# Experts: the order of a block's gate-and-up products with the high and low parts of the weights

## What is computed

```python
def expert_step(acc, ws):
    wgu, wd, g = ws
    a, b = jnp.split(x @ wgu, 2, axis=-1)
    return acc + g[:, None] * ((jax.nn.silu(a) * b) @ wd), None
```

## Time and profile before

| what | value |
|---|---|
| median of 3 runs | 1197.23 us (1196.26 to 1197.84) |
| the profiled execution's own time | 1197.68 us |
| its span, first to last instruction | 1195.8 us |
| experts' stage, first gate-and-up matmul to last down matmul | about 851.4 to 1160.1 us of the span |
| PE busy over the span | 1155.7 us, 97% |
| HBM traffic | 232.9 MB |

### The profile page before, as it was taken

One profiled execution on the slowest core, in us unless ns is written; L12 is line 12 of the kernel. 1 busy time (PEld: TensorE's weight loads), 2 busy tenths in 40 slices (PEclk: granted clock), 3 DMA queues, 4 the chain that ended last, 5 costly groups with the idle time before them and its releaser, 6 DMA issues. The chain is left out here.

```text
span 1195.8 us, 20090 instructions
## 1 busy us (share of the span) xinstructions
PE 1155.7 (97%) x7096; PEld 1018.7 (85%) x7096; DVE 716.3 (60%) x1262; ACT 597.8 (50%) x1006; POOL 87.2 (7%) x91
## 2 busy tenths in 40 slices
PE   8999999999999999999989999898799999999997
PEld 8999999899999989999979899687688888878862
DVE  3325255254453643535544765556898999989945
ACT  3233344333344334343365733313688888888952
POOL 0000000000000000000000000011222222222113
PEclk9999999999999999999999999898799999999999
DMA  6624316224252162522623333732699999999916
GB/s 200 168 77 120 104 56 168 75 75 133 69 149 76 53 166 75 145 70 62 168 64 105 89 106 120 278 117 111 238 373 358 357 348 368 380 364 370 367 55 263
DMA packets 178475, 210.50 MB, mean 176 GB/s; under 512 B 14054, under 2 KB 141543, under 8 KB 178428
## 3 DMA queue, kind: packets, MB, share of 16 engines
q1 hardware_dynamic: 155440, 188.07, 47.4%
q10 hardware_dynamic: 13644, 10.77, 2.8%
q0 software_dynamic: 9344, 11.03, 2.6%
HBM read 200.19 MB, written 32.71 MB: 195 GB/s over the span
## 5 line engine op out<-in xcount | busy, mean ns | idle before, releaser
L344 PE MATMUL bank_u<-x_hi,w_hi 128*128 128x320 f32 (+1 forms) x1024 | 326.6, 319 | 0.4 <-DVE x_lo L771 0.4
L345 PE MATMUL bank_u<-x_lo,w_hi 128*128 128x320 f32 (+1 forms) x1024 | 318.9, 311 | 0.0
L346 PE MATMUL bank_u<-x_hi,w_lo 128*128 128x320 f32 (+1 forms) x1024 | 318.0, 311 | 0.0
L344 PEld LDWEIGHTS bank_u<-x_hi,w_hi 128*128 128x128 f32 x1024 | 192.5, 188 | 8.7 <-issue 7.0
L345 PEld LDWEIGHTS bank_u<-x_lo,w_hi 128*128 128x128 f32 x1024 | 192.9, 188 | 0.0
L346 PEld LDWEIGHTS bank_u<-x_hi,w_lo 128*128 128x128 f32 x1024 | 192.8, 188 | 0.0
L766 DVE TENSOR_TENSOR w_lo<-w_raw,w_hi 128x1024 fp32r<-128x1024 f32 x80 | 97.8, 1222 | 147.8 <-ACT w_hi L544 147.3
L544 ACT CAST w_hi<-w_raw 128x1024 fp32r<-128x1024 f32 x80 | 83.4, 1043 | 45.6 <-issue 28.4
L1488 PE MATMUL banks<-w_hi_space,xT_hi 128*128 128x512 f32 x256 | 103.4, 404 | 2.0 <-issue 2.0
L1490 PE MATMUL banks<-w_hi_space,xT_lo 128*128 128x512 f32 x256 | 100.3, 392 | 0.0
L1489 PE MATMUL banks<-w_lo_space,xT_hi 128*128 128x512 f32 x256 | 100.3, 392 | 0.0
(11 more groups left out here) (282 smaller groups left out, 2140.8 us busy)
## 6 DMA issues: line engine op xcount, KB each, us to landing
w_raw<-in_w_in SPq DMA_DIRECT2D x64, 512.0 KB, 4.1
first_up<-in_w_gate_up SPq DMA_DIRECT2D x16, 2048.0 KB
second_up<-in_w_gate_up SPq DMA_DIRECT2D x16, 2048.0 KB
first_down<-in_w_down SPq DMA_DIRECT2D x16, 1024.0 KB
second_down<-in_w_down SPq DMA_DIRECT2D x16, 1024.0 KB
k_cache<-in_cache_k SPq DMA_DIRECT2D x16, 512.0 KB
v_cache<-in_cache_v SPq DMA_DIRECT2D x16, 512.0 KB
w_raw<-in_w_branch SPq DMA_DIRECT2D x16, 512.0 KB, 4.3
```

The lines of the kernel that those rows point to most:

```text
L344: pe.matmul(out, w_hi[:, u % 2, k, :], x_hi[:, k, cols], start=(k == 0), stop=False)
L345: pe.matmul(out, w_hi[:, u % 2, k, :], x_lo[:, k, cols], start=False, stop=False)
L346: last = pe.matmul(out, w_lo[:, u % 2, k, :], x_hi[:, k, cols], start=False, stop=(k == KT - 1))
```

## The change

In `gate_up` the 24 matmuls of a block are put into two passes over k. The first pass holds the two products with the high parts of the weights (16 matmuls) and waits for the high parts only (`up_hi_done`). The second holds the product with the low parts (8 matmuls) and waits for the low parts. `up_used` is now reported in the second pass, after the 18th, 20th, 22nd and 24th matmul of the block. No other engine's program is edited.

```diff
                 wait(pe, act_done, j - 1)
                 for k in range(KT):
                     if k % 2 == 0:
+                        pe.wait_ge(up_hi_done, 4 * j + k // 2 + 1)
+                    pe.matmul(bank_g[par][:], xT_hi[:, par, k, :], up_hi[:, k, :], start=(k == 0), stop=False)
+                    pe.matmul(bank_g[par][:], xT_lo[:, par, k, :], up_hi[:, k, :], start=False, stop=False)
+                for k in range(KT):
+                    if k % 2 == 0:
                         pe.wait_ge(up_lo_done, 4 * j + k // 2 + 1)
-                    pe.matmul(bank_g[par][:], xT_hi[:, par, k, :], up_hi[:, k, :], start=(k == 0), stop=False)
-                    pe.matmul(bank_g[par][:], xT_hi[:, par, k, :], up_lo[:, k, :], start=False, stop=False)
-                    last = pe.matmul(bank_g[par][:], xT_lo[:, par, k, :], up_hi[:, k, :], start=False, stop=(k == KT - 1))
+                    last = pe.matmul(bank_g[par][:], xT_hi[:, par, k, :], up_lo[:, k, :], start=False, stop=(k == KT - 1))
                     if k % 2 == 1:
                         last.then_inc(up_used, 1)
```

## The result

| | before | after |
|---|---|---|
| median | 1197.53 us (1196.26 to 1198.68, 4 runs) | 1211.31 us (1209.21 to 1211.47, 4 runs) |
| ratio to before | | 1.011, 95% interval 1.0097 to 1.0123 |
| profiled execution, its span | 1195.8 us | 1209.6 us |

The change makes the kernel slower by 13.8 us. The page of the kernel after, part 1, shows that the same instructions now stand in a longer span. PE has 43 us without work instead of 40, and its busy time grew by 10.9 us although the work is the same. Most of that growth is waiting that the modelled ends cover: in blocks 3 to 28 PE is shown busy for 253.22 us, where it was 247.10, at a granted clock of 1.00 both times.

A forecast was written before the change was run, and what follows sets the result against it. PE, 97% busy, bounds the kernel, with DVE, ACT and DMA nearly full. Block 0 +2.3, blocks 1-2 +0.3, 3-28 +7.7, 29 +0.2, 30 +0.8: +11.3 on 1197.23 gives 1208.5 us; range 1202 to 1214.

The forecast's parts named there:

- PE's work costs the same: In `gate_up`, matmuls and their weight loads stay, still spaced 0.227 us apart; costed at nothing.
- No gain from waiting for high parts: At the head of `gate_up`, waiting for high instead of low parts gives nothing, since PE never waits there.
- Cast 0 at +4.38: On ACT, the next block's quarter 0 is cast no earlier than 4.38 us after a block's first matmul; +3.22 before.
- 4.50 to `act_rows`, 0.47 to the turning: After the quarter 0 cast, DVE's `act_rows` follows 4.50 us later and PE's turning another 0.47 us later.
- Odd blocks 9.65: In the loop, odd blocks take 9.65 us, the next `gate_up` coming 0.30 us after the turning.
- Even blocks 10.17: In the loop, even blocks take 10.17 us, the next `gate_up` coming 0.82 us after the turning, at the branch.
- Blocks 0 to 2, +2.6: At the start of the experts' stage, block 0 grows by 2.3 us and blocks 1 and 2 together by 0.3.
- PE idle before the turning in some 30 blocks: Sign in the profile: PE's turning shown idle, waiting for `act_rows`, in some 30 blocks, where it was 3.
- The branch costs more than now, not the same: Rival at the loop's branch: cost no more than now, 8 passes or none; 1205.9 or 1201.7 us; chance 0.14.
- the rule on fetches: At the loop's branch: a taken branch breaks prefetch, far targets need a DMA fetch, so cost wouldn't follow PE's lateness.
- Late loads on top: Rival in the loop: weight loads become late again, 1217.3 us in all passes, about 1213 in half; chance 0.09.
- the faster case: Rival in blocks 3 to 28: late loads vanish and slack hides the new wait; 1193.9 us; chance 0.03.

The follow-up runs named there:

- e2: Changed kernel with the high parts of each quarter reported on their own, after the 4th, 8th, 12th and 16th matmul; 1197.33 us, ratio 1.0009.
- e7: Changed kernel with a separate high-part report, PE's blocks 3 to 28 written out, and `act_rows` behind quarters 0 and 1 on DVE; 1194.14 us, ratio 0.9976.
- e8: Kernel before with PE's blocks 3 to 28 written out and `act_rows` behind quarters 0 and 1 on DVE; 1194.66 us, ratio 0.9973.
- e5: Changed kernel with `act_rows` on DVE behind quarters 0 and 1 instead of 0 to 2; 1197.4 us, ratio 0.9992.
- e10: Kernel before, old matmul order, with `up_used` reported after the 21st, 22nd, 23rd and 24th matmul; 1229.85 us, ratio 1.0269.
- e3: Changed kernel with block 0 alone in the order, waits and reports of the kernel before; 1206.7 us, ratio 1.0084.
- e6: Kernel before with PE's program for blocks 3 to 28 written out instead of looped; 1195.94 us, ratio 0.9988.
- e4: Changed kernel with PE's program for blocks 3 to 28 written out instead of looped; 1201.44 us, ratio 1.0046.
- e1: Kernel before, old matmul order, with `up_used` reported after the 18th, 20th, 22nd and 24th matmul; 1210.2 us, ratio 1.0107.

## Why the prediction was right, and where it was off

The range (1202 to 1214) held the 1211.31 us, and the forecast case is the one that happened.

- *PE's work costs the same.* Right: matmuls start 0.227 us apart as before, and e2 shows the order alone at 1.0009.
- *No gain from waiting for high parts.* Right: e7 against e8 shows none even with late loads.
- *Cast 0 at +4.38.* Measured +4.40 to +4.43; the first ten matmuls of a block start up to 0.01 further apart than in the earlier trace rows.
- *4.50 to `act_rows`, 0.47 to the turning.* Measured 4.49 and 0.47 in all blocks. e5 and e10 move the two ends of this path one at a time, and the period follows.
- *Odd blocks 9.65.* Measured 9.67 (the 0.02 above). *Even blocks 10.17.* Measured 10.07: the pause was taken from block 4 alone, at 0.82; block 20, with 0.73, was nearer to the 0.69 that came. And the last pass has no jump back, so 12 pauses, not 13. Together the term of +7.7 came out as +6.4.
- *Blocks 0 to 2, +2.6.* This is the term that was mis-sized: +5.1. The step that failed was to give blocks 1 and 2 the path at full clock: the 2.75 us of waiting at the end of block 0 were not only a delay but also the idle time after which the clock fell (1.4 us in block 1). e3, without that wait, has no fall. The 0.8 us in block 0, ten matmuls at the low clock instead of six, are an accident of the execution: e3 and e6 have as many with the old order in block 0. The last 0.3 is block 2, 9.84 instead of 9.54: a pause where PE enters the loop, like that at the jump back. In e4, which has no loop on PE, block 2 takes 9.64.
- *Loads not late.* Right: no cast waited for a load.
- *PE idle before the turning in some 30 blocks.* This sign did not come: PE shows it twice and its weight load 24 times, since the modelled ends cover the wait. The starts show it in all of them, 0.47 after `act_rows`.
- *The rivals.* The branch costs more than now, not the same: its pause came in every pass that jumped back. The prediction set beside it the rule on fetches from the Trainium skill, "Runtime: NRT & Kernel Launch", section "Instruction fetch mechanics". By the trace the pause is no such fetch, since ten of the twelve fall in a stretch in which no instructions were fetched. With PE's lateness the pauses went from 8 to 12, and in e4 and e6 they went with the loop. Late loads on top did not occur, and the faster case fails on the cast at +4.4.

The sum was 1.3 us short in the blocks, of which the low clock in block 0 is 0.8, and the later start of the stage in this execution added 1.2 to the span. It came that near partly by luck: the loop was put 1.3 us too high and blocks 0 to 2 2.5 us too low. The central number was 2.8 us under the median. Of the four runs of the changed kernel only one was profiled, so whether the clock fell in the others isn't shown.

## What to carry to other kernels

When matmuls are put in another order, look first at what their completion gives back, and to whom: here a single-copy buffer was held for 12 matmuls more, and that cost 1.1% while the order itself cost nothing. Follow the freed buffer through the in-order queues to the item that the busiest engine waits for; the slack is the distance between that item and the moment it is wanted, and beyond it each microsecond counts in every iteration. If a pass needs only one part of an operand, report that part on its own, or move the item that is waited for ahead of the work that depends on the buffer.

## What the runs showed that was not expected

- In the changed kernel and in e1 the clock fell again after a wait of 2.75 us on PE, in e4 with the same wait it did not. In e10 it fell (granted clock 0.50) after a wait of 3.43 us. Each kernel was profiled once, so whether the fall comes and goes between executions of one kernel isn't shown.
- A jump back in PE's loop costs 0.5 us of a block (10.07 against 9.56 written out) once PE runs behind its waits, and even the blocks inside a pass lose 0.11 (9.67 against 9.56). A loop that is free while PE has work in hand is not free when it is late.
- The DMA engines moved 386 to 392 GB/s over 30 us at a share of 0.99 to 1.01.
- The moment at which the clock rises after the start of the stage differs by up to 2.4 us between the kernels' executions, which alone moves block 0 by 0.7 us (8.64 before, 9.31 in e6).
